# A decoder trunk on one core: tiles of the gated product spaced 2128 and 2060 bytes apart instead of 2048

## What is computed

```
def swiglu(h, w_gate, w_up, w_down):
    return (jax.nn.silu(h @ w_gate) * (h @ w_up)) @ w_down

x = x + 0.5 * swiglu(rmsnorm(x, norm_gain[layer, 0]), ...)
```

## Time and profile before

| | |
|---|---|
| median of 3 runs | 2073.67 us |
| profiled execution: span | 2072.4 us |
| profiled execution's own time against the median | the span is 1.3 us shorter |
| TensorE busy | 2052.6 us, 99% |
| VectorE busy | 1025.5 us, 49% |
| ScalarE busy | 779.5 us, 38% |
| GpSimd busy | 305.1 us, 15% |
| HBM read | 188.51 MB |

### The profile page before, as it was taken

One profiled execution on the slowest core, in us unless ns is written; L12 is line 12 of the kernel. 1 busy time (PEld: TensorE's weight loads), 2 busy tenths in 40 slices (PEclk: granted clock), 3 DMA queues, 4 the chain that ended last, 5 costly groups with the idle time before them and its releaser, 6 DMA issues.

```text
span 2072.4 us, 25759 instructions
## 1 busy us (share of the span) xinstructions
PE 2052.6 (99%) x9592; PEld 1704.6 (82%) x9592; DVE 1025.5 (49%) x1540; ACT 779.5 (38%) x1110; POOL 305.1 (15%) x390
## 2 busy tenths in 40 slices
PE   9999999999999999999999999999999999999998
PEld 7888888788888888888888888878888888888887
DVE  5444444488644444432444443266776544444423
ACT  5333322346743333322333322265565553333222
POOL 1000000354220000000000000047566010000000
PEclk9999999999999999999999999999999999999999
DMA  5323322354132333322333332223122132333331
GB/s 182 101 91 101 114 98 83 109 137 127 51 92 92 98 94 99 115 93 83 88 100 96 97 118 98 69 89 93 58 83 89 62 92 91 101 92 100 112 98 55
DMA packets 63100, 199.02 MB, mean 96 GB/s; under 512 B 12816, under 2 KB 14896, under 8 KB 63024
## 3 DMA queue, kind: packets, MB, share of 16 engines
q1 hardware_dynamic: 59616, 196.55, 30.3%
q10 hardware_dynamic: 3408, 1.44, 0.3%
HBM read 188.51 MB, written 2.38 MB: 92 GB/s over the span
## 4 chain that ended last, share of the span: by engine, by line
PE 92%; DVE 3%; ACT 2%; POOL 1%; issue 1%; DMA 1%; SPq 0%; ACTq 0%; DVEq 0%; POOLq 0%
PE prod L510 27%; PE prod L512 27%; PE prod L511 27%; PE misc L777 2%; PE misc L723 1%; PE prod L574 0%; PE prod L575 0%; PE prod L578 0%; ACT L1215 0%; PE misc L657 0%; PE misc L713 0%; PE prod L700 0%; POOL rows L1797 0%; PE prod L622 0%; PE prod L623 0%
## 5 line engine op out<-in xcount | busy, mean ns | idle before, releaser
L1275 DVE TENSOR_TENSOR w_lo<-raw,w_hi 128x1024 fp32r<-128x1024 f32 (+1 forms) x290 | 383.2, 1321 | 737.6 <-ACT w_hi L940 737.1
L510 PE MATMUL prod<-h_hi,w_hi 128*128 128x512 f32 x1848 | 737.9, 399 | 2.6 <-DVE w_lo L1275 1.2
L512 PE MATMUL prod<-h_hi,w_lo 128*128 128x512 f32 x1848 | 721.2, 390 | 0.0
L511 PE MATMUL prod<-h_lo,w_hi 128*128 128x512 f32 x1848 | 720.1, 390 | 0.0
L940 ACT ACTIVATE w_hi<-raw 128x1024 fp32r<-128x1024 f32 (+1 forms) x316 | 354.8, 1123 | 542.8 <-PE prod L512 527.2
L510 PEld LDWEIGHTS prod<-h_hi,w_hi 128*128 128x128 f32 x1848 | 347.6, 188 | 74.8 <-issue 6.4
L512 PEld LDWEIGHTS prod<-h_hi,w_lo 128*128 128x128 f32 x1848 | 347.1, 188 | 73.9
L511 PEld LDWEIGHTS prod<-h_lo,w_hi 128*128 128x128 f32 x1848 | 347.8, 188 | 68.1 <-issue 1.7
L510 PE MATMUL prod<-a_hi,w_hi 128*128 128x512 f32 x682 | 265.3, 389 | 0.0
L511 PE MATMUL prod<-a_lo,w_hi 128*128 128x512 f32 x682 | 265.3, 389 | 0.0
L512 PE MATMUL prod<-a_hi,w_lo 128*128 128x512 f32 x682 | 265.3, 389 | 0.0
(11 more groups left out here) (306 smaller groups left out, 1860.7 us busy)
## 6 DMA issues: line engine op xcount, KB each, us to landing
raw<-in_w SPq DMA_DIRECT2D x252, 512.0 KB, 3.6
raw<-in_wd SPq DMA_DIRECT2D x64, 704.0 KB, 4.1
blk<-blocks SPq DMA_DIRECT2D x16, 256.0 KB
x<-in_x SPq DMA_DIRECT2D x8, 256.0 KB, 6.0
k_dup<-k_dup SPq DMA_DIRECT2D x8, 256.0 KB, 3.7
silu_g<-g_rows SPq DMA_DIRECT2D x7, 256.0 KB, 4.7
out<-y_out SPq DMA_DIRECT2D x12, 128.0 KB, 1.8
raw<-in_w SPq DMA_DIRECT2D x4, 256.0 KB, 6.1
```

The source lines that it names most:

```text
L510: pe.matmul(bank, wh, hi, start=first and k == 0, stop=False)
L511: pe.matmul(bank, wh, lo, start=False, stop=False)
L512: ins = pe.matmul(bank, wl, hi, start=False, stop=last and k == tiles_n - 1)
L1275: dve.tensor_tensor(w_lo[:, n % 2, 0:w], raw[:, n % 4, 0:w], w_hi[:, n % 2, 0:w].bitcast(F32), ALU.subtract).then_inc(lo_ready, 1)
```

## The change

The change gives each tile of `a_hi` 20 float32 values of room behind it and each tile of `a_lo` 3. The tensors are allocated with rows of 532 and 515 values, and the names `a_hi` and `a_lo` then stand for the first 512 of each row. Tiles are 2128 and 2060 bytes apart. `sq0` is placed at the end of `a_hi`, as before, which is 1760 bytes further on. All else is the same.

```
+A_HI_PAD, A_LO_PAD = 20, 3
...
         ffn = Plan()
-        a_hi, a_lo = ffn("a_hi", [FT, T], F32R), ffn("a_lo", [FT, T], F32R)
-
-        sq0 = nc.alloc_sbuf_tensor_at("sq0", [P, KT, T], F32, offset=region0 + FT * T * 4)
+        a_hi = ffn("a_hi", [FT, T + A_HI_PAD], F32R)[:, :, 0:T]
+        sq0 = nc.alloc_sbuf_tensor_at("sq0", [P, KT, T], F32, offset=ffn.at)
+        a_lo = ffn("a_lo", [FT, T + A_LO_PAD], F32R)[:, :, 0:T]
```

## The result

| | before | after |
|---|---|---|
| median of 3 runs | 2073.67 us | 2086.20 us |
| span of the profiled execution | 2072.4 us | 2084.2 us |
| ratio of times, 95% interval | | 1.0064 (1.0046 to 1.0082) |
| measured again (e9_after_again; 13 runs before, 4 after) | 2073.88 us | 2086.61 us, 1.0061 (1.0045 to 1.0078) |

The page after: TensorE's busy time is 10.8 us longer, the other engines' times are the same, and the chain is again 92% TensorE with 27% on each matmul line (one line further down now, L511 to L513).

A forecast was written before the change was run, and what follows sets the result against it. TensorE's matmul spacing was taken to bound the kernel. The span of 2072.4 us less 10.9 us from 2178 down-stage matmuls, other terms 0, gave 2061.5, or 2062.8 us as median; range 2054 to 2085 us.

The forecast's parts named there:

- What bounds the kernel: Whole kernel: TensorE is busy 99% of 2072.4 us, so only matmul spacing or TensorE waits move the end.
- The excess: Down stages: 13.3 ns a matmul beyond its columns, 29.0 us over 2178 matmuls, claimed to be movable.
- Rival 1: Down-stage matmuls: addresses don't matter, only timing between stream and load; no change, 2073.7 us, chance 0.17.
- the value of the spacing: 2178 down-stage matmuls: excess taken as 8.3 ns instead of 13.3, bounded between 3 and 20 ns.
- the term that stood at -10.9 us: Spacing of the 2178 down-stage matmuls: 5.0 ns less each, the only term of the sum that was not 0.
- meet again and again: Down stages: streams at equal places start together and meet every time; new offsets put them apart for most tiles.
- The pair at 115 ns: Two matmuls of 256 columns after other side work, 0.23 us together, excess 8.3 ns; source of the value taken.
- Rival 2: Four down stages: streams at unequal places never settle, 4.4 ns more a matmul, +9.6 us, 2083.3 us; chance 0.33 with half forms.
- the unsettled run of the earlier trace: First gate stage before the change: nine spacings of 231.1 ns behind a float32 sum, before settling at 226.7.
- The range: Whole time, 8 in 10: 2054 to 2085 us, leaving out mean excesses under 4.3 ns and over 18.5.
- The covers: Down stages: slower writes of `a_hi` and `a_lo` would fall into idle time, TensorE reading 8.3 us later; 0 us.
- The register arithmetic: Tile addresses in the loop on VectorE (69 ns) and ScalarE: perhaps another form, in idle time, 0 us.

The follow-up runs named there:

- e9_after_again: The changed kernel as it is, timed again against the kernel before: 2086.61 us, ratio 1.0061 (1.0045 to 1.0078).
- e5: Down-projection matmuls alone over zeros, series of 48: all four operands or weights alone shifted, narrower weight loads, narrower streams; 226.7 ns a matmul at equal places with full loads.
- e4_map: Down-projection matmuls alone over zeros, 112 series of 48 with moving tiles or low weights at constant shifts; 226.7 ns unshifted, mean 233.6 over 63 common shifts.
- e6_search: Down-projection matmuls alone over zeros, 24 a series, operands at 240 random sets of places; cheapest 226.7 ns, dearest 238.2 ns a matmul.
- e7_pads: One output tile's 66 matmuls alone over zeros, exact layouts and all 300 padding pairs; 226.7 ns for the layout before, 233.2 for the changed one.
- e1_parts: Kernel before with another tile layout in each down stage: high tiles spaced 2128 bytes, low 2060, both interleaved, low 2064; 2080.16 us against 2073.44.

## Why the prediction was wrong

- **What bounds the kernel** was right: only TensorE's spacing moved the end, and the loss is in the four down stages.
- **The excess is not fixed and can be moved by the places** was right. Rival 1 would have left 226.7 ns; the change made 233.2. The Trainium skill, "TensorE: Matmul & The Clock Gate", Part 2 (LDWEIGHTS step), says that loading the next weights takes no read bandwidth from the running matmul. That may stand: e5 shows that a shorter load does not lower the excess (231.7 ns at 32 columns, 226.7 at 128), so no run here proves that the load is what disturbs the stream.
- **The step that failed is the value of the spacing**, "8.3 ns, the smallest that a pair at full rate shows". Measured is 233.15 - 213.3 = 19.8 ns, so the term that stood at -10.9 us is +13.0. The sign was lost in the sentence that the streams at equal places "meet again and again" and unequal ones would be apart. The runs show the contrary: over all 63 common shifts (e4_map), 240 random ones (e6_search) and all 299 paddings (e7_pads), none goes under equal places, and the 13.3 ns, read as a collision to get rid of, is the least that 512 columns cost here. The pair at 115 ns on which the value rested was the first after a change of shape. The next pair of the same rows already takes 0.24 us, 120 ns each, which is the settled value of 256 columns at equal places:

```profile
404.77 0.40 PE L657 MATMUL misc<-ik_dup,emix_lo 128*128 128x256 f32 x2
405.01 0.40 PE L510 MATMUL prod<-h_hi,w_hi 128*128 128x512 f32 x1
```

And it was of 256 columns, where e5 finds another order of places (116.7 at 16 bytes, 120.0 at equal). It should not have been carried to 512. The rows of 512 columns at hand, 231.1 ns on the way to the settled state, hinted at what leaving that state costs, and the prediction set them aside.
- **Rival 2** had the sign and the place: 2083.3 us forecast, 2086.2 measured. Its price was too small, 4.4 ns instead of 6.5, because the unsettled run of the earlier trace rows is one of equal places. Its last steps before 226.7 are 231, 236, 228, 233 and 231 ns, and in e5 the series at equal places, shifted together by 32, 64, 128 and 192 bytes, reach 226.7 by the same five, to 1 ns: it is a way into the settled state, not a sample of unequal places. The words of the rival are not quite right either: unequal places that stay constant do settle, each at its own dearer value (233.3, 240.0). The range ended at 2085.0, 1.2 us short. Its dear end was a mean excess of 18.5 ns, though the bound taken from the earlier trace rows was 20; the cut was made there without a row, and the measured 19.8 lay in what was cut.
- **The covers** held. The 88 writes take 632 and 693 ns (633 and 693 before), though their starts are no longer multiples of 2048, and TensorE waits for none of them. The register arithmetic did change its form on VectorE, 93 ns instead of 69, in idle time; on ScalarE it stayed at 51. The earlier trace rows are answered by

```profile
L1358 DVE TENSOR_TENSOR a_lo<-act_f,a_hi x88: 691/693/696, 31.5 to 1957.2; 128x512 f32 x78, 128x512 fp32r<-128x512 f32 x10
...
L1358 DVEq FUSED_REGOPS  x78: 93/93/105, 46.7 to 1934.8; - x78
```

- The page "SBUF — State Buffer" of the Trainium skill, with its note on 16-byte cachelines, was named against the low parts. Low tiles in whole 16-byte steps (e1_parts, stage 4, or e7's pair of 0 and 16 bytes at 231.1 ns) cost nearly what those at 12 bytes do (231.5), so crossing a line is not the price. The place inside a line does matter where both kinds share it (237.9 against 233.0 ns in e4_map).

What stays open is the mechanism under it: why the spacing depends on the distance to the weights and on the place inside 32 bytes, why a few unequal places are as cheap as equal ones, why a load of a quarter of the width leaves the excess, and why 256 and 384 columns rank the places otherwise. The runs show which layouts cost what, not why.

## What to carry to other kernels

In a dense chain of float32r matmuls of 512 columns, with weight loads of 128 columns, start every moving tile and every weight tile at the same place modulo 256 bytes, and that place at a multiple of 32 bytes; pad by multiples of 256 bytes if at all. The spacing is then 226.7 ns. At a common place of 4, 8 or 16 bytes it was 237.8, 232.3 and 230.0, and anywhere else it was nearly always 228 to 240. Before a layout is changed to get rid of an excess, ask whether the present one is the settled case: here, a few rows behind a disturbance showed a dearer state next to it. And a price must be taken from rows of the same shape; the order of the places was another at 256 columns.

## What had not been expected of the hardware

- A shift of the tiles by only 4 bytes is among the worst: 237.8 ns, and 240.0 at 68 bytes (e4_map), while 12 bytes past a 16-byte step is among the mildest (230.0 in the mean).
- Two disturbances together can cost less than their sum: 5.1 us a stage from the parts, 3.4 from both (e1_parts and the changed kernel, and the same in e7_pads without any other engine).
- The spacing is reproducible to the nanosecond: the pattern of 66 steps in the changed kernel is the same to 1 ns in every stage of both its profiled runs, and in e7_pads the same 66 steps, again to 1 ns, come from zeros in a kernel that does nothing else.
